# The pre-norm's 1/rms moved behind the up products, and down products that end bank by bank

## The reference, cut to what matters

```python
def _rmsnorm(x, g):
    y = x * lax.rsqrt(jnp.mean(x * x, axis=-1, keepdims=True) + RMS_EPS)
    return y * g

# first_block
h = _rmsnorm(x, norm_pre[0]);  x = x + _rmsnorm(ssd(h) @ w_out, norm_post[0])
h = _rmsnorm(x, norm_pre[1]);  x = x + _rmsnorm(attend(h @ w_q, _rmsnorm(mem, norm_mem) @ w_kv) @ w_o, norm_post[1])
h = _rmsnorm(x, norm_pre[2]);  x = x + _rmsnorm(conv_ffn(h @ w_up) @ w_down, norm_post[2])
# second_block
x = x + mixers(rmsnorm(x, norm1_g) @ w_in) @ w_o
x = x + conv_ffn(rmsnorm(x, norm2_g) @ w_up) @ w_down
return rmsnorm(x, final_g)
```

## Time and profile before

| | |
|---|---|
| median of 3 runs | 2893.8 us (2892.64 to 2895.66) |
| span of the profiled execution | 2889.6 us, 4.2 us below the median |
| TensorE matmuls busy | 2781.2 us (96%) |
| VectorE busy | 1633.0 us (57%) |
| ScalarE busy | 1330.6 us (46%) |
| GpSimd busy | 161.5 us (6%) |
| mean granted TensorE clock | 0.975 |

### The profile page before, as it was taken

How to read it: one execution, slowest core, us unless ns; L and a number is a source line. 1 busy time by engine, 2 the same in 40 slices (tenths; PEclk the granted TensorE clock), 3 DMA queues, 4 the chain that set the end, 5 groups by cost and what they waited for, 6 DMA issues and landing times. The chain is left out here.

```text
span 2889.6 us, 36004 instructions
## 1 busy us (share of the span) xinstructions
PE 2781.2 (96%) x13209; PEld 2322.3 (80%) x13209; DVE 1633.0 (57%) x1931; ACT 1330.6 (46%) x1587; POOL 161.5 (6%) x123
## 2 busy tenths in 40 slices
PE   7999999999978999999999989999999999999998
PEld 6888888878866888888788878877778888887886
DVE  4577777675465555555544455455455555555444
ACT  4455554444365544444443454342355444454343
POOL 1111111110010000000000010000000000000000
PEclk9899999999989999999999999997999999999999
DMA  6555555536533555555555466640445555555552
GB/s 212 177 165 189 179 188 186 188 145 237 189 131 113 194 186 181 184 187 185 187 197 189 160 199 186 196 160 1 175 148 188 189 178 186 187 189 188 189 190 101
DMA packets 222833, 505.45 MB, mean 175 GB/s; under 512 B 15234, under 2 KB 51122, under 8 KB 202026
## 3 DMA queue, kind: packets, MB, share of 16 engines
q1 hardware_dynamic: 218778, 479.98, 49.8%
q0 software_dynamic: 3984, 24.50, 2.4%
HBM read 499.12 MB, written 5.32 MB: 175 GB/s over the span
## 5 line engine op out<-in xcount | busy, mean ns | idle before, releaser
L1435 DVE TENSOR_TENSOR w_lo<-raw,w_hi 128x2048 fp32r<-128x2048 f32 (+3 forms) x472 | 1038.4, 2204 | 1001.5 <-ACT w_hi L640 989.3
L640 ACT ACTIVATE w_hi<-raw 128x2048 fp32r<-128x2048 f32 (+3 forms) x472 | 869.7, 1844 | 1223.7 <-PE PB L1020 824.0
L1018 PE MATMUL PB<-w_hi,hT_hi 128*128 128x512 f32 (+2 forms) x2656 | 1019.5, 384 | 3.7 <-DVE hT_lo L1464 2.8
L1020 PE MATMUL PB<-w_hi,hT_lo 128*128 128x512 f32 (+2 forms) x2656 | 1007.3, 379 | 0.0
L1019 PE MATMUL PB<-w_lo,hT_hi 128*128 128x512 f32 (+2 forms) x2656 | 1006.2, 379 | 0.0
L1018 PEld LDWEIGHTS PB<-w_hi,hT_hi 128*128 128x128 f32 x2656 | 505.3, 190 | 94.5 <-issue 3.1
L1020 PEld LDWEIGHTS PB<-w_hi,hT_lo 128*128 128x128 f32 x2656 | 504.6, 190 | 92.9
L1019 PEld LDWEIGHTS PB<-w_lo,hT_hi 128*128 128x128 f32 x2656 | 505.5, 190 | 90.4 <-issue 1.7
L1062 PE MATMUL PB<-w_hi,hT_hi 128*128 128x512 f32 x560 | 152.2, 394 | 5.0 <-ACT big L655 2.2
L1062 PE MATMUL T<-w_hi,hT_hi 128*128 128x512 f32 x560 | 149.8, 389 | 1.3 <-ACT big L776 1.3
L1062 PE MATMUL PB<-w_lo,hT_hi 128*128 128x512 f32 x560 | 150.0, 390 | 0.0
(11 more groups left out here) (257 smaller groups left out, 1732.9 us busy)
## 6 DMA issues: line engine op xcount, KB each, us to landing
raw<-in_ffn_w_up_dram SPq DMA_DIRECT2D x88, 1024.0 KB, 5.0
raw<-in_w_up_dram SPq DMA_DIRECT2D x88, 1024.0 KB, 5.0
raw<-in_ssd_w_in_dram SPq DMA_DIRECT2D x64, 1024.0 KB, 5.3
raw<-in_ffn_w_down_dram SPq DMA_DIRECT2D x44, 1024.0 KB, 4.8
raw<-in_w_down_dram SPq DMA_DIRECT2D x44, 1024.0 KB, 4.9
raw<-in_w_in_dram SPq DMA_DIRECT2D x40, 1024.0 KB, 5.0
raw<-in_ssd_w_out_dram SPq DMA_DIRECT2D x32, 1024.0 KB, 4.8
raw<-in_ssd_w_in_dram SPq DMA_DIRECT2D x64, 256.0 KB, 3.2
```

What stands on the lines that cost most here:

```text
L640: nc.scalar.activation(dst, src, ACT.Copy).then_inc(hi_ready, 1)
L1018: nc.tensor.matmul(o, h, wh[:, c, :], start=(k == 0), stop=False)
L1020: ins = nc.tensor.matmul(o, l, wh[:, c, :], start=False, stop=(k == KC - 1))
L1435: V.tensor_tensor(dst, src, h.bitcast(F32), ALU.subtract).then_inc(lo_ready, 1)
```

## The change

1. The pre-norm's 1/rms is no longer applied ahead of the transposes. x itself (and the memory) is transposed, block by block as the additions finish, and `evac` multiplies the product's rows by 1/rms with a per-token scale operand, after waiting for `rstd_done`. GpSimd's diagonal, the scaled copy and the waits for both go. The squares of x move behind the making of hT on ScalarE, and their sums behind h_lo on VectorE. The softmax scale that sat in the evacuation of the queries moves to VectorE's copy of them.
2. The last unit of each down product does quads 0 and 1 as before, then quads 2 and 3 together bank by bank, each bank with a count of its own (`bank_done`). The squares and additions wait for single banks. While tile 1's banks end, blocks 1, 2 and 3 of tile 0 of x are transposed between them; block 0 follows at the head of the next unit. Tile 0 is multiplied in the order of blocks 1, 0, 2, 3, since blocks 1 and 0 lie in PB 0 and 1, which the product itself writes.
3. GpSimd's queue: the spill of x no longer stands behind x's power, but its power now stands between the spill and the small loads.

```diff
-DIAGONAL = [(n, tt) for n in TRANSPOSED for tt in range(TT) if n not in BY_TILE or tt == 0]
-POST = [N_P1, N_P2, N_P3]
+FIRST_TILE_ORDER = (1, 0, 2, 3)
+FIRST_TILE_BANK = (1, 0, 2, 3)
...
+                at = FIRST_TILE_BANK[b]
+                return PB[at], ph_full[at], ph_empty[at], BY_TILE.index(n)
...
+        def x_count(k, tt, nb):
+
+            return ((k - 1) * TT + tt) * NB + nb + 1
+
+        def acc_landed(engine, k, unit, tt, nb):
+
+            if tt == TT - 1 and nb == NB - 1:
+                engine.wait_ge(quad_used, 4 * unit)
+            else:
+                engine.wait_ge(bank_done, (TT * NB - 1) * (k - 1) + tt * NB + nb + 1)
...
-            inverse_roots(N_P3, N_1)
+            inverse_root(N_P3)
             pool.wait_ge(x_new, 3 * TT * NB)
             pool.dma_start(x_d, x[:, :]).then_inc(x_spilled, 16)
+            inverse_root(N_1)
 
             pool.wait_ge(x_spilled, 16)
+            pool.wait_ge(sq_done, sq_count(N_1, TT - 1))
...
-            def evac(q, pair, dst, n=BLK, func=ACT.Copy, scale=1.0):
-
+            def evac(q, pair, dst, norm, n=BLK, func=ACT.Copy):
+
+                act.wait_ge(rstd_done, nth(norm, TT - 1))
                 act.wait_ge(quad_used, q + 4)
                 for tt in range(TT):
-                    ins = nc.scalar.activation(dst[:, tt, 0:n], PB[2 * pair + tt][:, 0:n], func, scale=scale)
+                    ins = nc.scalar.activation(dst[:, tt, 0:n], PB[2 * pair + tt][:, 0:n], func, scale=rstd(norm)[:, tt:tt + 1])
                 ins.then_inc(proj_evac, 1)
...
             def after_down(unit, post, n, k, gain, k0, scratch=xn_big):
@@ -714,19 +716,17 @@
                 if post is not None:
                     square_sums(post, k, unit, 0)
                 hi_unit(unit, js=(0, 1))
-                square_residual(n, k, 0, scratch)
-                hi_unit(unit, js=(2,))
-                act.wait_ge(quad_used, 4 * unit)
-                h_hi(n, 0, gain, k0)
+                h_hi(n, 0, gain, k0, None, FIRST_TILE_ORDER[0:1])
                 if post is not None:
                     square_sums(post, k, unit, 1)
-                hi_unit(unit, js=(3,))
-                square_residual(n, k, 1, scratch)
-                act.wait_ge(rstd_done, nth(n, 1))
-                for nb in range(NB):
-                    s = slice(nb * BLK, (nb + 1) * BLK)
-                    nc.scalar.activation(scratch[:, 1, s], xt[:, 1, s], ACT.Copy, scale=rstd(n)[:, 1:2]).then_inc(xn_ready, 1)
+                act.wait_ge(quad_used, 4 * unit)
+                h_hi(n, 0, gain, k0, None, FIRST_TILE_ORDER[1:2])
+                for j in (2, 3):
+                    hi_unit(unit, js=(j,))
+                    h_hi(n, 0, gain, k0, None, FIRST_TILE_ORDER[j:j + 1])
                 h_hi(n, 1, gain, k0)
+                for tt in range(TT):
+                    square_residual(n, k, tt, scratch)
...
                 by_tile = norm is not None and norm[0] in BY_TILE
@@ -1026,19 +1026,19 @@
                     _, _, empty, uses = h_bank(norm[0], tt, j)
                     pe.wait_ge(empty, uses + 1)
 
-                if norm is not None and not turned:
-                    norm_transposes(norm[0], norm[1], (0,))
                 if norm is not None and not by_tile:
-                    norm_transposes(norm[0], norm[1], (1,))
+                    if not turned:
+                        norm_transposes(norm[0], norm[1], 0)
+                    norm_transposes(norm[0], norm[1], 1)
                 if evac_before is not None:
                     pe.wait_ge(proj_evac, evac_before)
                 if by_tile:
-                    for j in range(4):
+                    norm_transposes(norm[0], norm[1], 0, FIRST_TILE_ORDER[1:2])
+                    for j in FIRST_TILE_ORDER:
                         split(0, j)
                         pe.wait_ge(lo_ready, q + j + 1)
-                        products(j, (0,))
-                        if j == 1:
-                            norm_transposes(norm[0], norm[1], (1,), norm[2])
+                        products(j, (0,), FIRST_TILE_ORDER[0], FIRST_TILE_ORDER[3])
+                    norm_transposes(norm[0], norm[1], 1, (0, 1))
                 for j in range(4):
                     if norm is not None:
                         split(1, j)
@@ -1046,19 +1046,21 @@
                         pe.wait_ge(lo_ready, q + j + 1)
                     ins = products(j, (1,) if by_tile else (0, 1))
                     ins.then_inc(quad_used, 1)
+                    if by_tile and j == 0:
+                        norm_transposes(norm[0], norm[1], 1, (2, 3))
...
+                def first_unit(q, xq, last):
+                    for tt in range(TT):
+                        free[tt]()
+                        for j in range(2 if last else 4):
+                            if tt == 0:
                                 operands(q, xq, j)
-                            ins = tile(j, tt, first, last)
-                            if m == 1:
+                            ins = tile(j, tt, True, last)
+                            if tt == 1:
                                 ins.then_inc(quad_used, 1)
-                            elif first and after and j in after:
+                            elif after and j in after:
                                 after[j]()
-                        if last and m == 0:
-                            ins.then_inc(tile0_done, 1)
+                        if last:
+                            by_bank(q, xq, tt, True)
+
+                def last_unit(q, xq):
+                    for tt in range(TT):
+                        for j in range(2):
+                            if tt == 0:
+                                operands(q, xq, j)
+                            ins = tile(j, tt, False, True)
+                            if tt == 1:
+                                ins.then_inc(quad_used, 1)
+                        by_bank(q, xq, tt, False)
+
+                def by_bank(q, xq, tt, first):
+
+                    if tt == 0:
+                        operands(q, xq, 2)
+                        operands(q, xq, 3)
+                    for nb in range(NB):
+                        end = tt == TT - 1 and nb == NB - 1
+                        ins = tile(2, tt, first, True, (nb,))
+                        if end:
+                            ins.then_inc(quad_used, 1)
+                        tile(3, tt, first, True, (nb,)).then_inc(quad_used if end else bank_done, 1)
+                        if then is not None and tt == TT - 1 and not end:
+                            norm_transposes(then, xt, 0, ((1, 2, 3)[nb],))
...
+            def norm_transposes(n, src, tt, banks=range(4)):
+
+                for b in banks:
+                    bank, full, empty, uses = h_bank(n, tt, b)
+                    if uses:
+                        pe.wait_ge(empty, uses)
+                    if n == N_MEM:
+                        pe.wait_ge(mem_landed[tt], 16)
+                    elif n == N_X:
+                        pe.wait_ge(x_landed[tt], 16)
+                    else:
+                        pe.wait_ge(x_new, x_count(BY_TILE.index(n) + 1, tt, max(b, FIRST_TILE_BANK[b]) if tt == 0 else b))
+                    for c in range(4):
+                        k = 4 * b + c
+                        ins = nc.tensor.transpose(bank[:, c * P:(c + 1) * P], src[:, tt, k * P:(k + 1) * P], ident[:, :])
+                    ins.then_inc(full, 1)
 
...
+            def after_down(unit, k, post, scale, n, gain, k0):
+
+                def added(tt):
+                    if post is None:
+                        product_added(tt, k, unit, xn_big)
+                    else:
+                        branch_added(post, tt, k, scale)
+
+                if post is not None:
+                    branch_mean(post, 0, scale)
+                added(0)
+                lo_unit(unit, js=(0,))
+                h_lo(n, 0, gain, k0, FIRST_TILE_ORDER[0:1])
+                lo_unit(unit, js=(1,))
+                h_lo(n, 0, gain, k0, FIRST_TILE_ORDER[1:2])
+                if post is not None:
+                    branch_mean(post, 1, scale)
+                for j in (2, 3):
+                    lo_unit(unit, js=(j,))
+                    h_lo(n, 0, gain, k0, FIRST_TILE_ORDER[j:j + 1])
+                added(1)
+                h_lo(n, 1, gain, k0)
                 for tt in range(TT):
                     bank_sums(n, tt)
                     mean(n, tt, D)
```

More of the change, by code:

```diff
@@ L660, in square, with h_hi @@
                 nc.scalar.activation(scratch, src, ACT.Square, accum_out=ssq(n)[:, tt:tt + 1]).then_inc(sq_done, 1)
-            def h_hi(n, tt, gain, k0, quads=None):
-                for b in range(4):
+            def h_hi(n, tt, gain, k0, quads=None, banks=range(4)):
+                for b in banks:
                     if quads is not None:
@@ L1006, in up, with products @@
             def up(q, pair, n, evac_before, after=None, norm=None, turned=False):
-                def products(j, tt):
```

(13 more changed lines are left out.)

151 lines of the change are left out of this document (51 added, 100 removed).

## The result

The changed kernel takes 2870.65 us (median of 4 runs, 2866.21 to 2872.14), the kernel before 2894.51 us on the same chip (2892.64 to 2895.66). The ratio is 0.9915, 95% interval 0.9903 to 0.9928: 23.9 us faster. Forecast were 2864.3 us, 29.5 us faster, with a range of 2853 to 2880.

The account below looks back on a forecast made before the run. TensorE, working nearly throughout, bounds the kernel; only its waits and droppable work can be won. Terms 10.8 + 8.0 + 6.6 + 6.1 + 1.8 + 1.8 - 5 - 0.6 = 29.5 us: 2893.8 to 2864.3, range 2853 to 2880.

Parts of the forecast that it names:

- The chain inside the boundary: At the boundaries behind wout, xo, dn1, wo2: shortened to 47.9, 43.2, 47.9, 42.7 us, saving 8.0, 10.8, 6.1, 6.6 us.
- Plain transposes: In the pre-norms, a tile's 16 transposes take 1.8 us instead of 3.73, saving 1.9 us of TensorE per diagonal tile.
- the pointer: In the evacuations, a pointer scale costs 0.1 us each, mostly hidden by ScalarE under products; 0.6 us lost.
- Bank by bank: In a down product's last unit, tile 0's banks end 1.36 us apart; squares done at 0.9 instead of 2.6 us.
- The clock: At the boundaries, six waits of 2.4 us and more lower TensorE's clock: 5 us lost, between 0 and 9.
- The spill: Behind dn1, small loads wait for the spill of x, landing at 40.4 us; boundary 47.9 for 54.0, 6.1 us saved.
- Tile 0 of x at the start: At the start, cheaper transposes of x's tile 0, in the middle of TensorE's work, save 1.8 us.
- A: Rival: the whole kernel follows the sum of the terms, 2857 to 2872 us; chance 0.52.
- B: Rival: each boundary keeps its idle time and saves only transposes, 3.5 us; 2877 us, from 2873 to 2884; chance 0.18.
- C: Rival: earlier, denser work keeps the clock from 88 to 106 us, and boundaries might not dip; 2851 us; chance 0.12.
- D: Rival: the evacuation's pointer scale is on the path, 16 us lost; 2880 us, from 2876 to 2887; chance 0.09.
- F: Rival: slower, clock falls to half over a long stretch of products; 80 us at half clock gives 2904; chance 0.05.

Follow-up runs that it names:

- run 1: The changed kernel with idle waits of TensorE at the four boundaries filled by matmuls whose result is never read: 2865.29 us.
- run 3: The changed kernel with ScalarE's eight squares of the new residual moved ahead of the split of tile 1's blocks 2 and 3: 2854.55 us.
- run 6: The changed kernel with the evacuations' scale an immediate 1.0 in place of the pointer to 1/rms: 2871.92 us.
- run 5: The changed kernel with each down product's last unit ending quad by quad again, the next transposes of tile 0 behind the whole unit: 2887.09 us.
- run 9: The changed kernel itself, unaltered, measured once more on another chip: 2874.22 us.
- run 10: The kernel of run 5 (changed kernel, endings quad by quad again), once more: 2882.35 us in one run.
- run 2: The changed kernel with dummy fp32 matmuls of 128 columns in four waits of the start: 2867.81 us.
- run 4: The changed kernel with VectorE's wait for the third stage's small loads moved to ahead of the first instruction that reads one: 2867.88 us.
- run 7: The changed kernel with both the edits of run 3 (squares ahead) and run 4 (later wait for the small loads): 2850.18 us.
- run 11: The kernel of run 7 once more, beside the changed kernel on the same chip: 2850.16 us.

## Why the prediction came out as it did

**The chain inside the boundary was right, but for dn1.** Forecast without clock 47.9, 43.2, 47.9, 42.7; measured with the clock kept up 48.0, 43.5, 48.0, 43.2 (run 1). The waits forecast at 2.4 and 2.8 us were 2.2 and 2.7. VectorE's queue (w_lo and h_lo of quads 2 and 3 ahead of the additions of tile 1) and ScalarE's (squares behind h_hi) stand where the forecast put them, and run 3 shows the second as a cause and not only as a neighbour: with the squares moved, what was queued behind them came at once.

**Plain transposes, the end, the pointer.** 1.91 us for a tile where 1.8 was forecast; 1.8 us at the end; 92 ns for the pointer where 0.1 us was taken. These hold. The term of -0.6 us for the pointer is too small to be seen: leaving the pointer out gained nothing (run 6).

**Bank by bank.** The forecast had the squares end 1.7 us earlier. Taking that away cost 8.1 us in the four boundaries (run 5), so the step holds. By the stages the endings are worth 9 us with the end of the kernel, about half of the 19.6; the medians of this chip give the norm's part and the endings as 9 and 13 us (runs 5 and 9) or 13 and 8 (runs 10 and 9), so which of them is worth more is open.

**The clock was mis-sized.** The forecast took 5 us for six waits, 9 at most. Run 1 shows 4.9 us inside the boundaries (1.5, 1.6, 1.8 and 0), which alone uses up the term, and 5.4 us in the stretches behind the waits before the next unit (0.85, 2.0 and 2.5), for which nothing was left. About 10 us in the profiled execution, twice the value taken and just over its bound; with the stretches that other executions of the same code at xo did not have (runs 2, 4 and 6) it is less. This is the term that was missed by most. The forecast counted six waits, of 2.4 us and more; the profile has seven with half clock behind them, some of only 2.2 us, and behind dn1 there was one for each of the two waits. In spans the forecast of 29.5 us was 9.9 too high: 5 by this term, 1 by the chains, 1.8 by tile 0 of x at the start and 0.5 by the rest of the start, and the remaining 1.3 us lie between the boundaries, most of them behind dn1.

**The spill was the wrong cause.** The forecast had the small loads "wait for the spill of x", and took 12.5 us for its landing, 11 to 14 at the bounds. It landed in 6.6 us. In the changed order it runs while no weights are loaded (308 GB/s in all), where before it ran beside them (331 GB/s in all) and took 12.2; the forecast's 12.5 count from the start of its issue and not, as it says, from the end, from where they are 11.9. That "both powers stand in front of the loads but are done by then" failed too: the second power ended last and released the loads. That power ended at 41.9 us from tile 1, where the forecast had both powers at 40.3, just ahead of the spill's 40.4. So the forecast of 47.9 us was right only because two of its chains ended within 0.1 us of each other, and the one that it named was not the one that held. To shorten the spill would have won nothing here by this reading; the squares won 4.4 us.

**Tile 0 of x at the start.** The block is 1.8 us shorter, but the span to the first boundary is not (795.23 and 795.76). The same code gave 795.8 and 799.0 us in two executions, and 794 to 801 us over all kernels, with the number of half-clock stretches before 120 us and between 606 and 657 us, so a difference of 2 us can't be read from one profile of each. One thing speaks for the change as the cause: between 77 and 111 us the kernel before has 17.1 us at half clock, and all eleven profiles with the new transposes and no dummies there have 23.9 to 30.7 us, the one with dummies 20.5. At half clock TensorE, busy throughout, loses half of that time, 3 to 7 us for 7 to 14 us more. With one profile of before this isn't shown. Whether the 1.8 us are in the total stays open, as does what sets these stretches.

**Which rival.** A came true. B (waits only exchanged) is what happened behind dn1: there the idle time stayed (11.5 and 10.8 us) and the gain was 4.2 us, near B's 3.5, though not by the chain that B names. At wo2 the idle time stayed too, and 5.2 of the 6.1 us are shorter busy time. At wout and xo 5.3 and 5.5 us of idling went, which B excludes. Neither half of C came: there were dips at the boundaries, and the long half clock near the start grew from 17.1 us. D is refuted by run 6. F's condition, 59 us more at half clock, is not met: 144.2 us before and 141.9 us after.

**The sum.** In spans: 25.5 (boundaries) less 5.9 (between them) is 19.6, as measured. The medians differ by 23.9: the profiled execution of before was a fast one, its span 4.9 us below the median of 2894.51, that of after 0.6 us below its own of 2870.65. So of the 23.9 us in the medians some 4 are spread between executions, and that brought the result nearer to the forecast of 29.5, which is luck. The forecast set the whole distance between span and median to overhead and should have taken part of it as spread.

## What to carry to other kernels

When a wait is shortened, count the clock for what remains: here waits of 2.2 us and more could each still bring a half-clock stretch, 1.7 us, so the gain was the chain's less that, and not the same in each execution. Before naming a DMA as the cause of a late load, look at the instruction directly ahead of it in its queue; a landing time read in one order does not hold in another, where other loads run beside it. And when an operation is moved off the critical chain, look for the idle time of its engine inside that chain: eight squares put there instead of behind it were worth 13 to 16 us, over half of the whole change.

## What the runs showed of the hardware

- The same spill of 2 MB landed in 12.2 us beside loads of weights (331 GB/s in all) and in 6.6 us alone (308 GB/s).
- Half clock of 17 to 31 us stands around the first products of x (64 columns), TensorE being busy without a gap in all but its first 6 us; filling the waits ahead of it did not remove it (20.5 us in run 2). In the attention of the third stage there are 44 to 58 us more, in every profile.
- A wait of 2.2 us may or may not bring half clock behind it. With the changed kernel's code at xo it did in three of five executions (the two of the changed kernel and run 2; not in runs 4 and 6). One program had it at wout and not behind dn1 in one execution (run 7) and the other way round in another (run 11).
- Two executions of the changed kernel agreed within 0.2 us at each boundary and differed by 3.3 us ahead of the first, by stretches at half clock. Two executions of two other programs (runs 5 and 10, runs 7 and 11) differed by 0.6 to 1.6 us at single boundaries, where their clock records differ too. So distances between fixed events repeat to 0.2 us where the clock record is the same, and to 1.6 us here where it isn't; the spans ahead of the first boundary do not repeat to less than 3.
